# Modulation slots spread over four column groups of TensorE

## The reference, cut to what matters

```python
sh1, sc1, g1, sh2, sc2, g2 = jnp.split(
    (jax.nn.silu(c) @ ada_w[layer] + ada_b[layer])[:, None, :], ADA_CHUNKS, axis=-1)
csh1, csc1, cg1, csh2, csc2, cg2 = jnp.split(
    jax.nn.silu(c_ctx) @ ada_w[layer] + ada_b[layer], ADA_CHUNKS, axis=-1)
...
h = modulate(rmsnorm_2(x, norm1_g[layer]), sh1, sc1)
```

## Time and profile before

| | us |
|---|---|
| median of 3 runs | 3328.54 |
| lowest, highest | 3309.85, 3331.75 |
| profiled execution, its own time | 3324.8 |
| its span, first to last instruction | 3323.0 |
| TensorE busy | 3224.5 (97%) |
| VectorE busy | 1690.0 (51%) |
| GpSimd busy | 1507.5 (45%) |
| ScalarE busy | 956.0 (29%) |
| mean granted clock of TensorE | 0.984 |

### The profile page before, as it was taken

How to read it: one execution, slowest core, us unless ns; L and a number is a source line. 1 busy time by engine, 2 the same in 40 slices (tenths; PEclk the granted TensorE clock), 3 DMA queues, 4 the chain that set the end, 5 groups by cost and what they waited for, 6 DMA issues and landing times.

```text
span 3323.0 us, 40136 instructions
## 1 busy us (share of the span) xinstructions
PE 3224.5 (97%) x15308; PEld 2090.9 (63%) x15452; DVE 1690.0 (51%) x3482; ACT 956.0 (29%) x1463; POOL 1507.5 (45%) x790
## 2 busy tenths in 40 slices
PE   7999999998999999998999899999999999999998
PEld 6887785687557887886777544566665444444444
DVE  6433696647554344002641799544442065555555
ACT  2011225523443002112412322333333332222222
POOL 4664479456003665464556533433333343333331
PEclk9998998999999999998999999999999999999999
DMA  3222122022322323132022444344444575555552
GB/s 137 101 99 82 71 82 55 10 91 81 119 102 78 114 84 111 74 114 86 20 101 102 152 152 152 144 189 190 187 189 192 182 245 202 202 202 202 202 202 76
DMA packets 139832, 429.99 MB, mean 129 GB/s; under 512 B 8640, under 2 KB 79424, under 8 KB 116544
## 3 DMA queue, kind: packets, MB, share of 16 engines
q1 hardware_dynamic: 125216, 353.40, 30.0%
q10 hardware_dynamic: 7200, 68.68, 5.0%
q0 software_dynamic: 7296, 6.31, 0.8%
HBM read 358.10 MB, written 73.40 MB: 130 GB/s over the span
## 4 chain that ended last, share of the span: by engine, by line
PE 88%; DVE 9%; ACT 1%; issue 1%; DMA 1%; POOL 0%; SPq 0%; DVEq 0%; ACTq 0%; POOLq 0%
PE bank L1030 13%; PE bank L1031 13%; PE bank L1032 13%; PE bank L612 3%; PE bank L607 3%; PE bank L608 3%; PE bank L1053 3%; PE bank L735 3%; PE bank L640 3%; PE bank L635 3%; PE bank L636 3%; PE bank L859 3%; PE bank L854 3%; PE bank L855 3%; PE bank L753 2%; PE bank L543 2%
## 5 line engine op out<-in xcount | busy, mean ns | idle before, releaser
L2345 POOL TENSOR_TENSOR work<-ring,work 128x4096 bf16<-128x4096 f32 x64 | 532.3, 8318 | 900.7 <-ACT work L1477 900.7
L1031 PE MATMUL bank<-work 128*128 128x512 bf16 x2004 | 760.0, 379 | 11.3 <-POOL work L2345 9.1
L1030 PE MATMUL bank<-work 128*128 128x512 bf16 x2005 | 760.3, 379 | 5.8 <-DVE work L2185 2.8
L1032 PE MATMUL bank<-work 128*128 128x512 bf16 x1991 | 755.1, 379 | 2.3
L2369 POOL CAST w_parts<-ring 128x1024 fp32r<-128x1024 f32 (+3 forms) x212 | 228.3, 1077 | 745.4 <-DMA ring<-in_wstream 177.1
L2371 POOL TENSOR_TENSOR w_parts<-ring,w_parts 128x1024 fp32r<-128x1024 f32 (+3 forms) x212 | 524.3, 2473 | 17.0
L2185 DVE TENSOR_TENSOR work<-hF,work 128x512 bf16<-128x512 f32 x128 | 308.0, 2407 | 250.6 <-ACT work L1561 247.4
L1030 PEld LDWEIGHTS bank<-work 128*128 128x128 bf16 x2048 | 200.6, 98 | 246.2 <-issue 12.7
L1032 PEld LDWEIGHTS bank<-work 128*128 128x128 bf16 x2048 | 200.5, 98 | 242.1 <-issue 0.8
L1031 PEld LDWEIGHTS bank<-work 128*128 128x128 bf16 x2048 | 200.5, 98 | 234.8 <-issue 0.6
L1477 ACT ACTIVATE work<-ring 128x4096 bf16<-128x4096 f32 x64 | 231.5, 3617 | 205.6 <-PE bank L1032 177.9
(11 more groups left out here) (329 smaller groups left out, 5186.6 us busy)
## 6 DMA issues: line engine op xcount, KB each, us to landing
ring<-in_wstream SPq DMA_DIRECT2D x128, 2048.0 KB, 7.7
hidden<-hF ACTq DMA_DIRECT2D x32, 1024.0 KB, 3.9
gates<-work ACTq DMA_DIRECT2D x16, 2048.0 KB, 8.3
hF<-hidden SPq DMA_DIRECT2D x32, 1024.0 KB, 7.0
work<-gates SPq DMA_DIRECT2D x32, 1024.0 KB, 10.4
rpb_tiles<-in_rpb POOLq DMA_DIRECT2D x192, 16.0 KB, 2.4
work<-rpb_tiles POOLq DMA_DIRECT2D x24, 128.0 KB, 2.5
ring<-in_wstream SPq DMA_DIRECT2D x5, 512.0 KB, 4.1
```

The source lines that it names most:

```text
L1030: pe.matmul(out, a(0), b(0), start=(start and k == 0), stop=False)
L1031: pe.matmul(out, a(0), b(1), start=False, stop=False)
L1032: mm = pe.matmul(out, a(1), b(0), start=False, stop=(stop and k == n - 1))
L2345: nc.gpsimd.tensor_tensor(SPLIT[:, p, 1, :], ring[:, p, :], SPLIT[:, p, 0, :], ALU.subtract).then_inc(lo, 1)
```

## The change

Feature tile k of a modulation slot is put into column group k % 4: its two result rows come to partitions 32 (k % 4) and 32 (k % 4) + 1 of the same bank instead of partitions 0 and 1. Tiles 0 to 3 begin the sums of their groups, tiles 4 to 7 end them, so that eight rows of partial sums stand in the bank. The copy to SBUF takes all 128 partitions; its two targets, `C_ROW` and `FILL_ROW`, grow from 2 partitions to 128. The four transposes become four f32 products of 128 x 128 by 128 x 2 with a small matrix `pick`, whose column c is one where the partition's number is c modulo 32, so that turning and adding of the partial sums are one product. `pick` is made once by VectorE at the start, as its first operation, from the identity. The places of the slots, the waits and the loads stay as they were.

```diff
--- before.py
+++ after.py
@@ -148,6 +148,7 @@
         rs = sb("rs", [P, 2, S])
         ada = sb("ada", [P, 2, 48])
         small = sb("small", [P, 512])
+        pick = sb("pick", [P, 2])
         WORK = 32900
 
         def rounded(name, at, *shape):
@@ -359,8 +360,8 @@
                           lambda t, h: B_V[:, t, h * 64:(h + 1) * 64],
                           B_Z, lambda qt, n: B_BIAS[:, qt, 0:n], 64 ** -0.5, "b")
         C_MASK = area(2048, S)
-        C_ROW = area(2560, S)[0:2, :]
-        FILL_ROW = rs[0:2, 1, :]
+        C_ROW = area(2560, S)
+        FILL_ROW = rs[:, 1, :]
         c_att = Attention(C_FREE, 0, 96, 1, 2,
                           lambda t, w: C_QKT[:, t, w, :], lambda t, w: C_QKT[:, t, 16 + w, :],
                           lambda t, h: C_VT[:, t, h * 64:(h + 1) * 64],
@@ -537,17 +538,18 @@
                     pe.wait_ge(signal("silu_c"), 1)
                     if m:
                         pe.wait_ge(signal("ada_taken"), m)
-                sc = silu_c.rearrange("p (k s) -> p k s", s=2)
                 w = slot_view(n % 2, KT, 512)
                 for k in ks:
-                    mm = pe.matmul(bank[0:2, b, :], sc[:, k, :], w[:, k, :], start=(k == 0), stop=(k == KT - 1))
+                    group = slice(32 * (k % 4), 32 * (k % 4) + 2)
+                    mm = pe.matmul(bank[group, b, :], silu_c[:, 2 * k:2 * k + 2], w[:, k, :], start=(k < 4), stop=(k >= 4))
                 if ks[-1] == KT - 1:
                     mm.then_inc(slot_used[n % 2], 1)
 
             def turn_modulation(m, b, row):
                 pe.wait_ge(signal("ada_row"), m + 1)
                 for j in range(4):
-                    mm = pe.transpose(bank[:, b, 2 * j:2 * j + 2], row[:, j * P:(j + 1) * P], ident[0:2, 0:2])
+                    mm = pe.matmul(bank[:, b, 2 * j:2 * j + 2], row[:, j * P:(j + 1) * P], pick[:, :],
+                                   start=True, stop=True)
                 mm.then_inc(signal("ada_turned"), 1)
 
             def turn_fill(tag, n):
@@ -1933,7 +1935,7 @@
             def take_row(m, b, row):
                 n = AT["ada", m]
                 dve.wait_ge(slot_used[n % 2], n // 2 + 1)
-                v.tensor_copy(row, bank[0:2, b, :]).then_inc(signal("ada_row"), 1)
+                v.tensor_copy(row, bank[:, b, :]).then_inc(signal("ada_row"), 1)
 
             def take_modulation(m, b):
                 b0 = COLS["ada_b"][0]
@@ -2199,6 +2201,7 @@
                                            in1=xF[:, k, :], op0=ALU.mult, op1=ALU.add).then_inc(signal("v_added"), 1)
                     squares_behind("final", k)
 
+            order(v.reduce_sum(pick[:, :], ident.rearrange("p (g c) -> p c g", g=4)[:, 0:2, :], AX))
             order(v.tensor_copy(posf[:, :], posi[:, :]))
             tables((32, "inv32", 0))
             for k in range(1, KT - 1):
```

## The result

The changed kernel takes 3278.34 us as the median of seven runs, the kernel before on the same chips 3315.2 us: a ratio of 0.9899 with a 95% interval of 0.9864 to 0.9934, some 33 us or 1.0%. The medians lie 36.9 us apart; the ratio goes by the fast runs alone, without one run of 3827.14 us of the kernel before. Two later comparisons gave 0.9905 (0.9888 to 0.9921) and 0.9885 (0.9862 to 0.9909).

A forecast was written before the change was run, and what follows sets the result against it. TensorE was taken as the bound, busy 97% of the span with 88% of the chain. Products 19.0 plus fills 4.2 less turning 7.8 gave 15.4 us off the 3328.5 us median: 3313 us, range 3294 to 3338.

The forecast's parts named there:

- The products in four groups: Modulation slots on TensorE: with starts in order, 9 pitches each, taken as 2.7 us less, 19.0 us in seven attention slots.
- bound by the input: TensorE in a slot: two f32 streams need no more input than one rounded stream, so two at once, not readily four.
- four at once: Rival for the slots: each group has its own queue, 4 pitches (1.72 us) a slot, 33.5 us won, 3295 us; chance 21%.
- its signs: Signs of four column groups running together in the second attention: 1.7 to 2.2 us a slot, heads of 10.5 us.
- The fills: Modulation pieces in the norms: b and c win 1.95 us each, a1 at most 0.28, d1 and d2 nothing; 4.2 us.
- the sign of being wrong: Norm b: its following group starts earlier, but its rests are waited for longer than 0.1 us.
- The turning: After each slot, eight f32 instructions replace four transposes: 0.65 us more, 12 times, 7.8 us lost, all of it counting.
- Copies, pick and ring: VectorE's result copy on 128 partitions, its small operation at the start, and SP's seven loads: no added time.
- The clock rival: Second attention: packed slots leave the clock at 1.2 GHz through seven heads, 90 us more, 3403 us; chance 4%.
- The rule of the Trainium skill: Weight loads on TensorE: column groups share rows, so no load overlaps and a slot keeps 6.88 us; the prediction doubted it.

The follow-up runs named there:

- the transposes: Changed kernel with the turning by four 128 x 128 transposes, VectorE adding the groups and no pick: 0.9898 of the kernel before, median 3279.89 us.

## Why the prediction was wrong

**The products in four groups** is the step that failed, at "if TensorE starts in order, the first of k+1 can start with the second of k". It gave 9 pitches a slot, in fact 4 and a tenth of a microsecond. The sum had 2.7 us a slot, and 5.14 were won (6.96 to 1.82), 17 us more over the seven heads. No row of the kernel before showed two groups together, and I let an order of starts stand in for a measurement. The trace after and the tiles in another order show that no instruction waits for a group that is not its own, with up to twelve ahead of it. My bound by the input was wrong too: four f32 streams run side by side at the full pitch of 0.43 us each, twice the input of a rounded product. The rival "four at once" had the mechanism and the size: 33.5 us against some 33 measured, and its signs came one by one (1.82 us a slot, heads of 10.5). I gave it 21%, and the range cut off its lower half.

**The fills** follow from the same step. b and c were to stay clear of VectorE's first rests and win 1.95 each; with four groups they run up against them and win 2.96 and 2.28. TensorE waits 0.31 us for the first rest of norm b, more than the 0.1 us named as the sign of being wrong. a1 gains 0.27 us (forecast at most 0.28), d1 and d2 0.06 and 0.07 (forecast nothing): there VectorE is last, as forecast. The rival's 2.7 for b came from a wrong reading of the kernel before. There TensorE reached the first rests not at some 263.45, as 261.3 and 2.15 give, but at 263.69, which is 3.0 us behind the 260.69:

```profile
263.69 2.03 PE L663 MATMUL bank<-w_parts,rest 128*128 128x512 f32 x8
```

**The turning** was a little dear: 0.65 us more was the sum's, 0.58 in the attention and 0.47 (c 0.54) in the norms were measured, 6.5 us in all instead of 7.8. The kernel with one group shows it alone: 0.61 us a head, and a loss against before. All of it lies on the path, as forecast; that does not mean that a shorter one is won in full, as the transposes showed.

**Copies, pick and ring**: the copy of 128 partitions takes 0.69 us for 0.68, the pick 0.17 us, TensorE has no wait in the seven heads, the loads come in time. Nothing, as forecast.

**The clock rival** did not come: 1.00 through all heads with a slot. Window of the changed kernel over the seven:

```profile
850.01:923.44 73.43, 73.43 (x491) 45.80 (x491) 45.52 (x165) 40.67 (x104) 6.80 (x4) 1.00 0.53 191
```

**The rule of the Trainium skill** on weight loads (TensorE: Matmul & The Clock Gate, Part 3, that they overlap products in flight only where the row group differs) is not borne out: all groups here share their rows, and eight loads go within 0.11 us, four more at each pitch while four products stream. The same part's table gives 2.38 times for three column groups; here four gave 6.96 / 1.82 = 3.8 times and two gave 2.0.

**The place of the range.** The sum stood on a median of 3328.5 of three runs; over seven it is 3315.2. The forecast's own 15.4 us against that would have been 3300, and the four at once 3282, with 3278 measured. A range set in microseconds takes in this shift, a ratio does not. But it is not what put the time outside: moved down by the same 13.3 us, the range would begin at 3281, still above 3278.

## What to carry to other kernels

Products with few result rows, put into different column groups, cost as much as the group with the most work: count instructions per group, not in all. Here six tiles took 1.81 us and eight 1.82, because the fullest group has two in both. Their order in the list does not matter, as far as it was tried. What joins the parts afterwards stands where the products stood and was paid in full. Read a mean over all the stages that a change touches: five heads of seven hid what the last one gave back. Where short work fills TensorE's pauses, it can also be what keeps its clock: look at the granted clock behind it before it is moved.

## What the runs showed of the hardware that I had not expected

Four f32 products of 128 x 2 by 128 x 512 ran side by side, 16 in 1.82 us, in either order. A piece of four tiles in four groups costs 0.97 us before the next work, one tile alone 0.95. Two single tiles, 0.86 us of pitch each, decided in norm b whether the work behind them ran at 1.00 or at 0.55, the 1.2 GHz level for most of it; without them the clock fell at five of five norms, in the execution with the transposes as well at four of five. And the granted clock of the same kernel fell in different stretches in two executions (0.77 at 600 us, 0.69 at 350 us), worth some 6 us in the one that could be measured.
